# Layer-0 mixer slots: state update before the rest of the output, inversion before centring, output projection in two pieces

## What is computed

```python
def mixer_ab_layer(x, conv_buf, s_gdn, x_prev, s_rwkv, p):
    xn = rms_norm(x, p['norm0_w'])
    proj = xn @ p['w_in0']
    ...
    o_a, s_gdn_new = gated_delta_chunked(q, k, v, beta, logd, s_gdn)      # mixer A: 4 heads of 128
    o_a = rms_norm(o_a, p['gdn_norm_w']).reshape(bsz, L, A_VAL) * jax.nn.silu(z_a)
    ...
    o_b, s_rwkv_new = rwkv7_scan(rh, heads(jnp.exp(logw)), kh, vh, -kk, kk * heads(a), s_rwkv)  # mixer B: 8 heads of 64
    gmean = jnp.mean(o_b, axis=-1, keepdims=True)
    gvar = jnp.mean(jnp.square(o_b - gmean), axis=-1, keepdims=True)
    o_b = ((o_b - gmean) * lax.rsqrt(gvar + B_GN_EPS)).reshape(bsz, L, B_W)
    o_b = (o_b * p['rwkv_ln_w'] + p['rwkv_ln_b'] + bonus) * jax.nn.silu(gb)
    y = jnp.concatenate([o_a, o_b], axis=-1).astype(x.dtype) @ p['w_out0']
    return x + y, conv_new, s_gdn_new, xn[:, -1], s_rwkv_new
```

## Time and profile before

| | us |
|---|---|
| median of 3 runs (lowest, highest) | 2047.07 (2046.57, 2047.74) |
| the profiled execution: its own time | 2052.62 |
| its span in the trace | 2050.5 |
| the eight slots, first join to last projection | 462.4 |

### The profile page before, as it was taken

How to read it: one execution, slowest core, us unless ns; L and a number is a source line. 1 busy time by engine, 2 the same in 40 slices (tenths; PEclk the granted TensorE clock), 3 DMA queues, 4 the chain that set the end, 5 groups by cost and what they waited for, 6 DMA issues and landing times. The chain is left out here.

```text
span 2050.5 us, 32226 instructions
## 1 busy us (share of the span) xinstructions
PE 1781.7 (87%) x13399; PEld 1558.1 (76%) x13399; DVE 811.9 (40%) x1436; ACT 515.8 (25%) x1114; POOL 315.0 (15%) x266
## 2 busy tenths in 40 slices
PE   5999969999737799999998893999999995999985
PEld 3999959889727677777775762999999994777764
DVE  4445534655453455566564522300110104344332
ACT  4344432333311222222231233221111112111101
POOL 5122211112011011111211001221111102000000
PEclk7999989999966689899899867999999995888887
DMA  6022221320162233233242025232113105332114
GB/s 177 1 86 85 86 65 43 107 98 34 66 214 65 51 95 85 63 95 94 60 116 56 32 47 149 80 103 71 54 54 105 43 23 188 101 103 89 59 52 47
DMA packets 248647, 166.27 MB, mean 81 GB/s; under 512 B 90994, under 2 KB 230491, under 8 KB 248520
## 3 DMA queue, kind: packets, MB, share of 16 engines
q1 hardware_dynamic: 248520, 164.44, 28.5%
HBM read 106.51 MB, written 57.89 MB: 80 GB/s over the span
## 5 line engine op out<-in xcount | busy, mean ns | idle before, releaser
L1839 PE MATMUL c_bank<-c_wo,c_ot 128*128 128x512 f32 (+1 forms) x288 | 135.5, 631 | 7.6 <-ACT c_ot L1361 7.6
L2451 DVE SCALAR_TENSOR_TENSOR e_t<-e_t,e_bank 128x512 f32<-128x512 f32 (+1 forms) x20 | 12.6, 632 | 288.3 <-ACT e_t L2404 288.3
L85 PE MATMUL e_bank<-e_wp0h,e_xh 128*128 128x256 f32 x432 | 122.5, 283 | 2.0 <-issue 2.0
L85 PE MATMUL e_bank<-e_wp1h,e_xh 128*128 128x256 f32 x432 | 122.3, 283 | 0.0
L86 PE MATMUL e_bank<-e_wp1l,e_xh 128*128 128x256 f32 x432 | 122.3, 283 | 0.0
L87 PE MATMUL e_bank<-e_wp0h,e_xl 128*128 128x256 f32 x432 | 122.3, 283 | 0.0
L86 PE MATMUL e_bank<-e_wp0l,e_xh 128*128 128x256 f32 x432 | 122.2, 283 | 0.0
L87 PE MATMUL e_bank<-e_wp1h,e_xl 128*128 128x256 f32 x432 | 122.2, 283 | 0.0
L1839 PEld LDWEIGHTS c_bank<-c_wo,c_ot 128*128 128x128 f32 (+1 forms) x288 | 55.6, 196 | 82.3 <-issue 80.9
L85 PEld LDWEIGHTS e_bank<-e_wp0h,e_xh 128*128 128x128 f32 x432 | 82.9, 192 | 2.2 <-issue 2.2
L85 PEld LDWEIGHTS e_bank<-e_wp1h,e_xh 128*128 128x128 f32 x432 | 82.9, 192 | 0.0
(11 more groups left out here) (567 smaller groups left out, 4755.8 us busy)
## 6 DMA issues: line engine op xcount, KB each, us to landing
k_w<-in_w_in_dram SPq DMA_DIRECT2D x33, 512.0 KB, 5.4
e_w<-in_w_in_dram SPq DMA_DIRECT2D x16, 1024.0 KB, 7.3
scratch_rw<-b_x SPq DMA_DIRECT2D x16, 544.0 KB, 2.7
scratch_qkv<-a_o SPq DMA_DIRECT2D x12, 544.0 KB, 5.5
e_xs<-scratch_xnT SPq DMA_DIRECT2D x8, 544.0 KB, 4.6
scratch_ql<-e_qb SPq DMA_DIRECT2D x8, 544.0 KB, 3.0
n_x<-in_x_prompt_dram SPq DMA_DIRECT2D x8, 512.0 KB, 7.6
c_ra<-scratch_rw SPq DMA_DIRECT2D x16, 256.0 KB, 3.7
```

The source lines that it names most:

```text
L85: pe.matmul(out, w[0], x[0], start=first, stop=False)
L1839: mm = pe.matmul(bank[c][0:T, :], OT[:, kt, 0:T], wo[:, kt, 512 * c:512 * c + 512], start=(kt == 0), stop=(kt == KT - 1))
L2451: dve.scalar_tensor_tensor(out=t2, in0=t2, scalar=1.0, in1=two(b, at), op0=ALU.add, op1=ALU.mult).then_inc(ev(f"free{b}"), 1)
```

## The change

Per engine, for slot i:

- PE: `out` is split into `out_state(i)` (the products with the states) and `out_rest(i)`, and `update(i)` goes between them. Then come `end_rows(i-1)`, now into banks 0 and 1, `rows_a` (the first half of `rows_ab`, now banks 2 and 3), the first half of the projection, `rows_b` (banks 4 and 5), `rows_vg`, the second half of the projection.
- DVE: `end_gate(i-1)`, five operations in one place after the scores, is split in three and spread over the slot; `invert(i+1)` moves ahead of `center`, `ends` and `decayed`.
- ACT: `copy_rows(i-1)` moves ahead of `out_a`, and `out_b` ahead of `values`.
- SP: `scatter` moves ahead of `load_rows`; `load_qk` waits for one more event, z5, which DVE signals after the second join.
- POOL: `norms(i)` runs at the end of slot i and not in slot i+1.

```diff
@@ sync
                 for i in range(TILES):
                     n, t = i + 1, i + 1
                     sp.wait_ge(ev("rhs_a"), n)
+                    sp.wait_ge(ev("z5"), n)
                     load_qk(t * P, size(t))
...
+                    scatter(t, 4 if t < TILES else 2)
                     if t < TILES:
                         sp.wait_ge(ev("rows_a"), t + 1)
                         sp.wait_ge(ev("rows_b"), t + 1)
                         sp.wait_ge(ev("rows_vg"), t + 1)
                         load_rows((t + 1) * P, size(t + 1))
-                    scatter(t, 4 if t < TILES else 2)
@@ gpsimd
-                    pool.wait_ge(ev("zw") if i else ev("gnw"), max(i, 1))
+                    pool.wait_ge(ev("rstd") if i else ev("gnw"), max(i, 1))
...
-                    if i >= 1:
-                        norms(i - 1, P)
                     products_of(i, P)
+                    norms(i, P)
@@ scalar
                     keep_sa(i, P)
+                    if i >= 1:
+                        copy_rows(i - 1, P, (0, 1))
                     out_a(i, P, 6)
                     keys(t, T)
-                    if i >= 1:
-                        copy_rows(i - 1, P, (4, 5))
+                    out_b(i, P)
                     values(t, T)
-                    out_b(i, P)
@@ vector
+                    if i >= 1:
+                        gate_scale(i - 1, P)
                     dve.wait_ge(ev("y6mm"), 2 * n)
...
+                    if i >= 1:
+                        gate_z(i - 1, P)
                     decay(t, T)
                     lower(t, T)
                     nv(i, P)
                     attention(t, T)
-                    scores(t, T, range(2, BH))
+                    scores(t, T, (2, 3))
                     if i >= 1:
-                        end_gate(i - 1, P)
+                        gate_bonus(i - 1, P)
+                    scores(t, T, range(4, BH))
                     state(i)
+                    invert(t)
                     center(i, P, 7)
                     ends(t, T)
                     decayed(t, T)
-                    invert(t)
                     end_sums(i, P)
@@ tensor
                     caus = K.causal if T == P else K.causal_s
                     pe.wait_ge(ev("xk"), max(t - 2, 0))
-                    pe.wait_ge(ev("vr_a"), t)
...
-                        pe.wait_ge(ev("ot"), max(t - 2, 0))
-                        pe.wait_ge(ev("state_a"), max(t - 1, 0))
-                        pe.wait_ge(ev("tt1"), max(t - 1, 0))
+                        pe.wait_ge(ev("krr"), t)
...
-                def rows_ab(t, T):
+                def rows_a(t, T):
                     pe.wait_ge(ev("ld_v"), 16 * (t + 1))
-                    pe.wait_ge(ev("sc"), 8 * t + 6)
+                    pe.wait_ge(ev("sc"), 8 * t + 8)
                     for h in range(AH):
-                        pe.transpose(v4(0, T)[:, h, :], QK[:, 1, h, 0:T], K.ident[:, :])
-                        mm = pe.transpose(v4(1, T)[:, h, :], V[:, h, 0:T], K.ident[:, :])
+                        pe.transpose(v4(2, T)[:, h, :], QK[:, 1, h, 0:T], K.ident[:, :])
+                        mm = pe.transpose(v4(3, T)[:, h, :], V[:, h, 0:T], K.ident[:, :])
                     mm.then_inc(ev("rows_a"), 1)
-                    pe.wait_ge(ev("sc"), 8 * t + 8)
+
+                def rows_b(t, T):
+                    pe.wait_ge(ev("state_a"), t)
+                    pe.wait_ge(ev("tt1"), t)
...
-                    out(i)
+                    out_state(i)
                     update(i)
-                    rows_ab(t, T)
+                    out_rest(i)
                     if i >= 1:
-                        pe.wait_ge(ev("state_a"), i + 1)
-                        pe.wait_ge(ev("tt1"), i + 1)
-                        end_rows(i - 1, P, (4, 5))
+                        pe.wait_ge(ev("sc"), 8 * t + 6)
+                        end_rows(i - 1, P, (0, 1))
+                    rows_a(t, T)
+                    if i >= 1:
+                        end_project(i - 1, P, 0)
+                    rows_b(t, T)
                     rows_vg(t, T)
                     if i >= 1:
-                        pe.wait_ge(ev("vr_a"), t + 1)
-                        for c in range(2):
-                            end_project(i - 1, P, c)
+                        end_project(i - 1, P, 1)
```

More of the change, by code:

```diff
@@ L1343, in _ @@
                         norm(i - 2, P)
-                    if i >= 1:
-                        norms(i - 1, P)
                     products_of(i, P)
+                    norms(i, P)
                 norm(TILES - 2, P)
-                norms(TILES - 1, P)
                 products_of(TILES, SR)
@@ L1389, in keys @@
                     act.wait_ge(ev("rows_a"), t + 1)
-                    act.activation(krs[t % 2][0:T, :, :], v4(0, T), ACT.Copy).then_inc(ev("kr"), 1)
-                    act.activation(vrs[t % 2][0:T, :, :], v4(1, T), ACT.Copy).then_inc(ev("vr_a"), 1)
+                    act.activation(krs[t % 2][0:T, :, :], v4(2, T), ACT.Copy).then_inc(ev("kr"), 1)
+                    act.activation(vrs[t % 2][0:T, :, :], v4(3, T), ACT.Copy).then_inc(ev("vr_a"), 1)
                 def values(t, T):
@@ L1396, in values @@
                     act.wait_ge(ev("upd_b"), t)
-                    act.activation(Br[0:T, :], bank[2][0:T, :], ACT.Copy, scale=-1.0).then_inc(ev("br"), 1)
-                    act.activation(Kr[0:T, :], bank[3][0:T, :], ACT.Copy).then_inc(ev("krr"), 1)
+                    act.activation(Br[0:T, :], bank[4][0:T, :], ACT.Copy, scale=-1.0).then_inc(ev("br"), 1)
+                    act.activation(Kr[0:T, :], bank[5][0:T, :], ACT.Copy).then_inc(ev("krr"), 1)
                     act.wait_ge(ev("rows_vg"), n)
@@ L1530, in end_sums, with gate_scale @@
                     dve.tensor_scalar(sm[0:T, 4:12], st[0:T, 4:12], 1.0 / 64, B_GN_EPS, ALU.mult, ALU.add).then_inc(ev("stats"), 1)
-                def end_gate(f, T):
+                def gate_scale(f, T):
                     n = f + 1
@@ L1540, in end_gate, with gate_z @@
                     dve.tensor_tensor(ob, ob, wide(rstd[0:T, 4:12], T, 64), ALU.mult).then_inc(ev("ob1"), 1)
+                def gate_z(f, T):
+                    n = f + 1
                     dve.wait_ge(ev("oa1"), n)
@@ L1543, in end_gate, with gate_bonus @@
                     dve.tensor_tensor(OR[0:T, 0:AKEY], OR[0:T, 0:AKEY], Z[0:T, :], ALU.mult).then_inc(ev("oa"), 1)
-                    o = OR[0:T, AKEY:D]
                     dve.wait_ge(ev("ob1"), n)
                     dve.wait_ge(ev("gw"), n)
-                    dve.tensor_tensor(o, o, gw[0:T, :], ALU.mult).then_inc(ev("ob2"), 1)
+                    dve.tensor_tensor(OR[0:T, AKEY:D], OR[0:T, AKEY:D], gw[0:T, :], ALU.mult).then_inc(ev("ob2"), 1)
+                def gate_bonus(f, T):
+                    n = f + 1
                     dve.wait_ge(ev("ob2"), n)
                     dve.wait_ge(ev("bv"), n)
-                    dve.tensor_tensor(o, o, bv[0:T, :], ALU.add).then_inc(ev("ob"), 1)
+                    dve.tensor_tensor(OR[0:T, AKEY:D], OR[0:T, AKEY:D], bv[0:T, :], ALU.add).then_inc(ev("ob"), 1)
+                def end_gate(f, T):
+                    gate_scale(f, T)
+                    gate_z(f, T)
+                    gate_bonus(f, T)
                 def end_add(f, T, c):
@@ L1890, in score @@
                               ).then_inc(ev("score"), 1)
[L1892 removed]
+                def rows_a(t, T):
                     pe.wait_ge(ev("ld_v"), 16 * (t + 1))
[L1894 removed]
+                    pe.wait_ge(ev("sc"), 8 * t + 8)
                     for h in range(AH):
[L1896 to L1897 removed]
+                        pe.transpose(v4(2, T)[:, h, :], QK[:, 1, h, 0:T], K.ident[:, :])
+                        mm = pe.transpose(v4(3, T)[:, h, :], V[:, h, 0:T], K.ident[:, :])
                     mm.then_inc(ev("rows_a"), 1)
[L1899 removed]
+                def rows_b(t, T):
+                    pe.wait_ge(ev("state_a"), t)
+                    pe.wait_ge(ev("tt1"), t)
                     for j in range(NP):
[L1901 to L1902 removed]
+                        pe.transpose(v4(4, T)[:, j, :], RB[:, 0, j, 0:T], K.ident[:, :])
+                        mm = pe.transpose(v4(5, T)[:, j, :], RB[:, 1, j, 0:T], K.ident[:, :])
                     mm.then_inc(ev("rows_b"), 1)
@@ L2007, in kd, with out_state @@
                         mm.then_inc(ev("rhs_b"), 1)
-                def out(i):
-                    n, sc = i + 1, SCs[i % 2]
+                def out_state(i):
+                    n = i + 1
                     pe.wait_ge(ev("qg"), n)
@@ L2018, in out, with out_rest @@
                     mm.then_inc(ev("rth"), 1)
+                def out_rest(i):
+                    sc = SCs[i % 2]
                     for h in range(AH):
@@ L2049, in _ @@
                     score(0, P, h)
-                rows_ab(0, P)
+                rows_a(0, P)
+                rows_b(0, P)
                 rows_vg(0, P)
```

4 lines of the change are left out of this document (1 added, 3 removed).

## The result

| | before | changed |
|---|---|---|
| median of 4 runs each (lowest, highest) | 2047.4 us (2046.57, 2057.98) | 1999.59 us (1996.97, 2005.78) |
| profiled execution: own time, span | 2052.62, 2050.5 | 1996.97, 1995.3 |

The ratio is 0.976, 95% interval 0.972 to 0.980: 47.8 us by the medians, where 38.4 were predicted (2008.7), within the range. Run again beside the kernel before on two other chips, the changed kernel gained 34.5 and 33.1 us (2040.59 to 2006.12, 2036.81 to 2003.69), ratio 0.983 both times. So the prediction lies between the first measurement and the two later ones.

A forecast was written before the change was run, and what follows sets the result against it. PE, busy 87% of the span, was taken to bound the kernel through its work, clock or waits. Gains of 5.1 + 16.1 + 7.5 + 9.7 = 38.4 us took 2047.07 to 2008.7 us; range 1989 to 2028.

The forecast's parts named there:

- slow join: Joins of a slot at low clock, with a PE idle gap; priced at 9.7 us per slow slot, three before.
- Slot 0: In slot 0, `invert` starts when its load lands, so c_x arrives 5.1 us earlier; bounds 3 and 6.
- The waits at the slots' ends: Slots 1 to 7: PE's waits for ACT's squares and copies, 19.3 us, shrink to 0.45 each; gain 16.1.
- The projections: Three of seven projections ran at lower clock behind stalls; all three slow stretches go, gain 7.5 us.
- first kind of slow stretch: Projections behind the 1.82 and 0.93 us stalls: two took 17.0 us, one 15.5, against 14.0 at clock 1.00.
- The rival "slower": Clock falls in every cut-up tail, all seven projections take 17.0 us, and joins may slow too; up to 2068.5; chance 0.05.
- The joins: Later `load_qk` traffic shrinks PE's gaps in the joins: two slow joins instead of three, gain 9.7 us.
- second kind: PE idle in the joins with nothing holding it: 1.09, 2.00, 1.47 and 0.63 us in slots 2, 3, 6, 7.
- The rival with one slow join: Only one slot's joins stay slow, where the forecast took two: 1999.0 us; chance 0.2.
- a risk for slot 7: 21 fewer PE semaphore instructions move packet borders, which can open a gap in a slot without one, slot 7 above all.
- An edit costed at nothing: `load_rows` issued later, behind `rows_vg`: free, since needed only behind the next slot's second join, over 20 us later.
- Three slow joins: Rival: as many slots with slow joins as before, since all now come closer on the last projection: 2018.4 us; chance 0.17.

The follow-up runs named there:

- the controls: The changed kernel itself, run twice more beside the kernel before on other chips: 2006.12 and 2003.69 us, ratio 0.983 both times.
- second control: The changed kernel with nothing altered, the later of two repeat runs: 2003.69 us, ratio 0.983 to the kernel before.
- first control: The changed kernel with nothing altered, the earlier of two repeat runs: 2006.12 us, ratio 0.983 to the kernel before.

## Why the prediction was right, and what was off

The mechanism is borne out term by term, but for a part of the joins. How near the total came (38.4 predicted; 47.8, 34.5 and 33.1 measured) is partly luck, since it moves by 9 to 10 us with each slow join, and their number differs from run to run.

- *Slot 0*: 5.1 predicted, 5.5 measured, and the load of c_ln does end the wait for the inversion, as worked out.
- *The waits at the slots' ends*: 16.1 predicted, 15.5 measured. The copies cost 0.30 to 0.39 us per slot (0.45). The error is slot 7: the centring's time was worked out for slot 1's queue, where it had 2.1 us to spare (1.0 in slot 3, as it turned out), and not for slot 7's, where the sample states' loads stand ahead of the triangles. That is 1.6 us, and by the run with the old order of products the update's place is what keeps this wait out of the other six.
- *The projections* (the prediction's first kind of slow stretch, those at 0.82 and 0.90 in the earlier trace rows): 7.5 and 7.5. All halves take 7.0 to 7.1 us. The rival "slower" (a clock that falls in the cut tail) did not occur: slots 2, 3 and 4 have 1.00 throughout. That a wait in that place does take the clock down is shown by the run with both halves together (first halves of 7.8 to 9.1 us, at 0.77 to 0.89). No run shows the next step of that rival, a tail at the lower level that hands it on to the joins: in that same run the second halves behind them stand at 1.00 again (7.03 us each), and in the kernel before slot 3's projection, at 0.62 up to 863.0 us, stands at 1.00 from there on, as do the joins of slot 4.
- *The joins* (its second kind), the term that was mis-sized: 9.7 predicted, 17.7 measured in the profile. "I take two slow joins instead of three"; it was one, and a quarter of another. The rival with one slow join (1999.0) is where the first measurement stood (1999.59); the controls at 2003.7 and 2006.1 had one and two, and gained 33 to 35 us, less than predicted. So the 8 us more are scatter as far as the runs show. The argument was right in part: the later `load_qk` alone, in the kernel before, gave 0.5% (some 10 us) and took one slow join of three away, as this term says, though its removal from the changed kernel cost at most 0.8% and perhaps nothing. What the term took too lightly are the borders. The prediction named them, as a risk for slot 7; with the changed kernel's borders slot 7 had no gap, in any of its three profiles, and slot 5 had one in all three. By the table that is what the move of 3 to 18 places does: the bad places were in slots 2, 6 and 7 (149, 241, 8), and came to be in slots 2, 5 and 6 (152, 230, 0). It gained no slot. Slot 3's gap of 2.00 us stood at a good place (172) and went with the later `load_qk` (0.39 in the run of that edit alone). Nor did the prediction price slot 1, which lasted 61.45 us at clock 0.79 before and 60.40 after; it lies behind slot 0's stalls in both.
- *An edit costed at nothing* that was not: `load_rows` later. It was judged by when its data are needed, over 20 us later, and that was right; but its traffic now ends in the next slot's joins, and slot 1, which had no gap before, got one of 0.8 to 1.6 us in each profile of the changed kernel. Since slot 1 is slow anyway, that cost little; with `invert` back, three other slots were slow with gaps, and the same effect is the likely reason.

What the borders cost, as measured: in the seven profiles of the table, slots whose first border lies at 26 or at 166 to 226 had gaps of 0 to 0.46 us, the others, but one of 0.37, gaps of 0.55 to 1.46, and 366 instructions that do nothing made the kernel 17 us faster by the medians (2007.41 to 1990.35). Three slow joins, the 2018.4 of the prediction, did not come in any of the changed kernel's three profiles (one, two and one).

How much of the 47.8 us each part is worth cannot be added up from the runs that undo one part: they give 23 (`invert`), 74 (`scatter`), 64 (the halves) and 19 (the products), 180 in all, and the 23 and the 19 hold slow joins, which scatter. The parts stand or fall together: each leaves PE the slack that the next one uses up. Left open is why the gaps differ from run to run at the same border (0.37 to 0.92 us at 152), and why PE idles longer with the border at some places than at others; only the borders' place was moved, not the kind of work around it.

The fastest version found is the one with fixed borders and the later weights' load: 1990.35 us, 13 us under the changed kernel. The fixed borders without the later load were not timed; in its profile 7.2 us of the prologue come from the load, and the slots are 12.1 us shorter than the second control's.

## What to carry to other kernels

Where TensorE runs hundreds of small matmuls back to back, look for idle time put down to "issue" and for what the clock does behind it: here, behind the gap of 1.45 us in slot 5 of the profile after, it stood at 0.50 from 890.6 to 907.7 us, and the slot took 57.92 us against 48.87. A few instructions that do nothing can move such gaps: here a slot of 1280 = 5 x 256 instructions made slots 2 to 6 alike, within 0.3 us and at clock 1.00. When a step moves in a queue, ask where its traffic ends as well as when its data are needed; here the later row loads went with a gap of 0.8 to 1.6 us in slot 1. Count the instructions to each gap: here all 63 stood 251 or 252 instructions behind a border, which ties them to the packets. And undo parts one at a time before believing a sum: a part costed at nothing may be what holds the others up.

## What was not expected of the hardware

A gap of about 1 us in the joins went with up to 10 us more for its slot, and its length does not tell whether it will: 0.89 us in slot 2 went with 58.6 us for the slot in the first control and with 49.8 in the run with early `load_qk`. A stall before a slot does it without any gap: slot 1 takes 59 to 62 us, behind slot 0, with a gap or without one, in every profile in which it has no new long wait of its own. And a load of 4 MB that nobody waits for held up a chain of one small load, the inversion and two stores by 7.2 us in the prologue.
